# Encoder layer on one core: the first up step in two parts, and another order of VectorE's work at both phase boundaries

## The reference

```python
h = rmsnorm(x, norm1_g); proj = h @ w_in          # q, k, v, u
a = block_swept_gqa(rope(q), rope(k), v)          # 8 query heads, 2 kv heads
p = multiscale_pool(u, w_pool, pool_scale)
x = x + jnp.concatenate([a, p], axis=-1) @ w_out  # phase "out"
h2 = rmsnorm(x, norm2_g)
x = x + jnp.square(jax.nn.relu(h2 @ w_up)) @ w_down   # phases "up" and "down", hidden width 4096
```

## Time and profile before

| | us |
|---|---|
| median of 3 runs | 1525.66 |
| the profiled execution | 1525.22 |
| its span | 1523.4 |
| PE busy | 1495.4 (98%) |
| DVE busy | 1024.2 (67%) |
| ACT busy | 718.8 (47%) |
| POOL busy | 384.4 (25%) |

### The profile page before, as it was taken

How to read it: one execution, slowest core, us unless ns; L and a number is a source line. 1 busy time by engine, 2 the same in 40 slices (tenths; PEclk the granted TensorE clock), 3 DMA queues, 4 the chain that set the end, 5 groups by cost and what they waited for, 6 DMA issues and landing times.

```text
span 1523.4 us, 23325 instructions
## 1 busy us (share of the span) xinstructions
PE 1495.4 (98%) x8011; PEld 1329.0 (87%) x8011; DVE 1024.2 (67%) x1285; ACT 718.8 (47%) x1212; POOL 384.4 (25%) x340
## 2 busy tenths in 40 slices
PE   9999989999999998999999999999999999999998
PEld 8999977888878887999999999999778888888887
DVE  7434489999975667445444544548788878878875
ACT  6323289998843434455455544546233223223220
POOL 3356358888950000000000000000311311311300
PEclk9999999999999999999999999999999999999999
DMA  6110021000055747532432433338743443443434
GB/s 238 42 38 18 18 85 34 14 11 10 15 174 179 255 145 296 213 136 110 153 133 103 149 124 126 132 140 311 258 141 100 147 155 96 149 154 97 148 99 177
DMA packets 68953, 195.19 MB, mean 128 GB/s; under 512 B 5528, under 2 KB 7712, under 8 KB 68768
## 3 DMA queue, kind: packets, MB, share of 16 engines
q1 hardware_dynamic: 66832, 183.36, 34.9%
q10 hardware_dynamic: 2064, 11.08, 1.8%
HBM read 119.97 MB, written 67.63 MB: 123 GB/s over the span
## 4 chain that ended last, share of the span: by engine, by line
PE 87%; DVE 4%; POOL 3%; issue 3%; ACT 2%; DMA 0%; ACTq 0%; POOLq 0%; DVEq 0%; SPq 0%
PE ps L754 22%; PE ps L755 22%; PE ps L756 22%; PE ps L1048 5%; PE ps L929 3%; PE ps L1058 3%; PE ps L911 2%; PE ps L913 2%; PE ps L944 2%; PE ps L945 2%; POOL prob L2186 1%; DVE yacc L2024 1%; PE ps L1068 1%; DVE pTlo L1595 1%; DVE nmax L1654 1%
## 5 line engine op out<-in xcount | busy, mean ns | idle before, releaser
L754 PE MATMUL ps<-h,wuhi 128*128 128x384 f32 x896 | 300.3, 335 | 4.8 <-issue 3.8
L756 PE MATMUL ps<-h,wulo 128*128 128x384 f32 x896 | 299.9, 335 | 0.0
L755 PE MATMUL ps<-h,wuhi 128*128 128x384 f32 x896 | 299.8, 335 | 0.0
L754 PE MATMUL ps<-wdhi,hidhi 128*128 128x512 f32 x672 | 262.3, 390 | 3.7 <-DVE yacc L2024 3.7
L755 PE MATMUL ps<-wdlo,hidhi 128*128 128x512 f32 x672 | 261.5, 389 | 0.0
L756 PE MATMUL ps<-wdhi,hidlo 128*128 128x512 f32 x672 | 261.5, 389 | 0.0
L2024 DVE TENSOR_TENSOR yacc<-yacc,ps 128x1024 f32<-128x1024 f32 x168 | 204.3, 1217 | 78.1 <-PE ps L756 77.6
L1155 ACT ACTIVATE hidhi<-hin 128x1024 fp32r<-128x1024 f32 (+1 forms) x72 | 86.8, 1205 | 308.9 <-PE ps L756 298.5
L1939 DVE TENSOR_TENSOR u<-u,ps 128x384 f32<-128x384 f32 x96 | 53.1, 553 | 185.3 <-PE ps L756 185.2
L754 PEld LDWEIGHTS ps<-h,wuhi 128*128 128x128 f32 x896 | 168.8, 188 | 5.6 <-issue 5.6
L755 PEld LDWEIGHTS ps<-h,wuhi 128*128 128x128 f32 x896 | 168.8, 188 | 0.0
(11 more groups left out here) (198 smaller groups left out, 2816.2 us busy)
## 6 DMA issues: line engine op xcount, KB each, us to landing
hd<-hout SPq DMA_DIRECT2D x64, 384.0 KB, 3.3
hin<-hd SPq DMA_DIRECT2D x48, 512.0 KB, 3.8
hd<-hout SPq DMA_DIRECT2D x32, 576.0 KB, 2.8
hin<-hd SPq DMA_DIRECT2D x24, 768.0 KB, 4.4
wuraw<-in_w_up SPq DMA_DIRECT2D x17, 1024.0 KB, 6.1
wdraw<-in_w_down SPq DMA_DIRECT2D x8, 2048.0 KB, 9.5
h<-h2d ACTq DMA_DIRECT2D x7, 1536.0 KB, 13.8
xin<-in_x SPq DMA_DIRECT2D x12, 512.0 KB, 3.5
```

Of the source, the lines that this page charges most:

```text
L754: pe.matmul(out, w_hi, m_hi, start=start, stop=False, skip_group_check=resumed)
L755: pe.matmul(out, w_hi, m_lo, start=False, stop=False, skip_group_check=resumed)
L756: return pe.matmul(out, w_lo, m_hi, start=False, stop=stop, skip_group_check=resumed)
```

## The change

- PE: products 2 and 3 of step 0 are made in two parts. The first two pairs (256 columns) of both run right after the last transposes (`up_first_pairs`); the third pair (128 columns) waits for `h2_lo` as the whole product did. The banks of the up steps are numbered anew, so that product 3's bank is not one that the last transposes are read from.
- DVE in phase out, p = 10: residual 10 comes after the four sums and before the five low halves of `lo_h2(9)`; the four `sum_wu` all come after the scaling. p = 11: only weight parts 2 and 3 are split before the scaling; part 4 after it; parts 5 and 6 after `lo_h2(11)`.
- DVE in the first unit of phase down: acc 2 comes before `lo_part(0, 2)` and `lo_part(1, 0)`.
- Last product: DVE adds its q = 0 half when PE has made the first six matmuls, then the other half; SP stores the two tiles of that quarter one by one.

ACT's and POOL's lists are unchanged.

```diff
@@ -315,6 +315,8 @@
         y_in = [sem(f"y_in{u}") for u in range(UNITS)]
         down_done = sem("down_done")
+        down_half = sem("down_half")
+        acc_half = sem("acc_half")
         acc_done = sem("acc_done")
         y_out = sem("y_out")
@@ -447,7 +449,7 @@
         OPENS = (0, 1, 3)
         GATHER = (0, 1, 0, 2, 0, 2, 0)
-        UP_BANKS = ((6, 7, 5), (2, 3, 4))
+        UP_BANKS = ((6, 7, 2), (3, 4, 5))
         QUARTERS = ((0, 0), (0, 0), (1, 0), (1, 1), (1, 1), (1, 0), (0, 1))
@@ -731,16 +733,21 @@
                 for half, h in ((0, 0), (1, 1), (1, 0), (0, 1)):
                     done = max(o for o in range(SLOTS) if QUARTERS[o] == (half, h))
-                    sp.wait_ge(acc_done, SLOTS * (UNITS * (DOWNS - 1) + u + 1) + done + 1)
+                    if (u, done) == (UNITS - 1, SLOTS - 1):
+                        sp.wait_ge(acc_half, 1)
+                    else:
+                        sp.wait_ge(acc_done, SLOTS * (UNITS * (DOWNS - 1) + u + 1) + done + 1)
                     a, b = unit_tiles(u, half)
                     cols = slice(h * 512, (h + 1) * 512)
-                    if b == a + 1:
+                    if b == a + 1 and (u, done) != (UNITS - 1, SLOTS - 1):
                         sp.dma_start(y[a * P:(a + 2) * P, cols].rearrange("(q p) n -> p q n", p=P),
                                      acc_quarter(u, half, h)).then_inc(y_out, 16)
                     else:
                         for j, t in enumerate((a, b)):
+                            if j and (u, done) == (UNITS - 1, SLOTS - 1):
+                                sp.wait_ge(acc_done, SLOTS * (UNITS * DOWNS + 1))
                             sp.dma_start(y[t * P:(t + 1) * P, cols], yacc[:, u, half, j, cols]).then_inc(y_out, 16)
-            sp.wait_ge(y_out, 16 * 4 * (UNITS + 1))
+            sp.wait_ge(y_out, 16 * (4 * (UNITS + 1) + 1))
@@ -1091,16 +1098,28 @@
                 if o == 6:
                     pe.wait_ge(u_sum, 3 * s + 2)
+                pairs = slice(2, 3) if isinstance(s, int) and s == 0 and o in (2, 3) else slice(0, 3)
+                up_pairs(g, par, o, pairs).then_inc(up_done, 1)
+
+            def up_pairs(g, par, o, pairs):
+
                 for k in range(4):
-                    mm = three(up_bank(par, o), wuhi[o][:, k], wulo[o][:, k], h2[g][o][:, 0, :, k], h2[g][o][:, 1, :, k],
-                               o in OPENS and k == 0, k == 3, o not in OPENS)
-                mm.then_inc(up_done, 1)
+                    mm = three(up_bank(par, o)[:, pairs], wuhi[o][:, k], wulo[o][:, k], h2[g][o][:, 0, pairs, k],
+                               h2[g][o][:, 1, pairs, k], o in OPENS and k == 0 and pairs.start == 0, k == 3, o not in OPENS or pairs.start > 0)
+                return mm
+
+            def up_first_pairs(o):
+
+                pe.wait_ge(wu_lo, o + 1)
+                if o == 2:
+                    pe.wait_ge(u_copied, 1)
+                up_pairs(1, 0, o, slice(0, 2))
             def up_step(s, w, g, par):
...
                     up_product(s, w, g, par, o)
-            def down_product(n, z, u, o):
+            def down_product(n, z, u, o, last):
                 m = UNITS * n + u
                 if u == 0:
@@ -1117,18 +1136,22 @@
                         mm = three(banks[:, q], hidhi[i][:, k, q, j], hidlo[i][:, k, q, j],
                                    wdhi[z][o][:, k], wdlo[z][o][:, k], o in OPENS and k == 0, k == 1, o not in OPENS)
+                    if q == 0 and (u, o) == (UNITS - 1, SLOTS - 1) and last:
+                        mm.then_inc(down_half, 1)
                 mm.then_inc(down_done, 1)
-            def down_chunk(n, z):
+            def down_chunk(n, z, last=False):
                 for u in range(UNITS):
                     for o in range(SLOTS):
-                        down_product(n, z, u, o)
+                        down_product(n, z, u, o, last)
             for p in range(TT):
...
             up_product(0, 0, 1, 0, 1)
             transpose_x2(TT - 1)
+            up_first_pairs(2)
+            up_first_pairs(3)
             for o in range(2, SLOTS):
                 up_product(0, 0, 1, 0, o)
@@ -1141,7 +1164,7 @@
                 down_chunk(h * 2 + 1, 1)
                 down_chunk(h * 2 + 2, 0)
-            down_chunk(DOWNS - 1, 1)
+            down_chunk(DOWNS - 1, 1, True)
@@ -1853,7 +1876,7 @@
                                          ).then_inc(xs2_done, 1)
-            def lo_h2(p):
+            def lo_h2(p, sums=True, halves=True):
                 q = p // 2
@@ -1864,20 +1887,26 @@
                     dve.wait_ge(h2_stored[2], 32)
                 raw = {o: h2_full(q, o) for o in (2, 3, 4, 5)}
-                dve.wait_ge(xT2_done, p + 1)
-
-                dve.wait_ge(h2_b11, q + 1)
-                dve.tensor_tensor(raw[4], h2_bank(q, 2), raw[5], ALU.subtract).then_inc(h2_sum, 1)
-                dve.wait_ge(h2_sum, 4 * q + 1)
-                dve.tensor_tensor(raw[2], h2_bank(q, 3), raw[4], ALU.subtract).then_inc(h2_sum, 1)
-                dve.wait_ge(h2_sum, 4 * q + 2)
-                dve.tensor_tensor(raw[3], raw[2], raw[5], ALU.subtract).then_inc(h2_sum, 1)
-                dve.wait_ge(h2_sum, 4 * q + 3)
-                dve.tensor_tensor(raw[5], h2_bank(q, 1), raw[2], ALU.subtract).then_inc(h2_sum, 1)
-                dve.wait_ge(h2_sum, 4 * q + 4)
-                for n, o in enumerate(LATE_HALVES):
-                    dve.wait_ge(h2_hi, SLOTS * q + 3 + n)
+
+                def half(o):
+                    dve.wait_ge(h2_hi, SLOTS * q + 1 + o)
                     minus(h2_half(q, o, 1), h2_bank(q, 3) if o == 6 else raw[o], h2_half(q, o, 0)).then_inc(h2_lo, 1)
+
+                if sums:
+                    dve.wait_ge(xT2_done, p + 1)
+
+                    dve.wait_ge(h2_b11, q + 1)
+                    dve.tensor_tensor(raw[4], h2_bank(q, 2), raw[5], ALU.subtract).then_inc(h2_sum, 1)
+                    dve.wait_ge(h2_sum, 4 * q + 1)
+                    dve.tensor_tensor(raw[2], h2_bank(q, 3), raw[4], ALU.subtract).then_inc(h2_sum, 1)
+                    dve.wait_ge(h2_sum, 4 * q + 2)
+                    dve.tensor_tensor(raw[3], raw[2], raw[5], ALU.subtract).then_inc(h2_sum, 1)
+                    dve.wait_ge(h2_sum, 4 * q + 3)
+                    dve.tensor_tensor(raw[5], h2_bank(q, 1), raw[2], ALU.subtract).then_inc(h2_sum, 1)
+                if halves:
+                    dve.wait_ge(h2_sum, 4 * q + 4)
+                    for o in LATE_HALVES:
+                        half(o)
             dve.wait_ge(pv_done, seqs[1].turn(NQ // 2, 0, 0))
@@ -1914,22 +1943,26 @@
                 if p + 1 < TT:
                     split_c(p + 1)
-                lo_h2(p - 1)
-                residual(p)
                 if p == TT - 2:
+                    lo_h2(p - 1, halves=False)
+                    residual(p)
+                    lo_h2(p - 1, sums=False)
                     lo_wu(0, 0)
                     lo_wu(0, 1)
-                    sum_wu(0, 0)
-                    sum_wu(0, 1)
+                else:
+                    lo_h2(p - 1)
+                    residual(p)
                 if p == TT - 1:
-                    for o in range(2, SLOTS - 1):
-                        lo_wu(0, o)
+                    lo_wu(0, 2)
+                    lo_wu(0, 3)
                 scale_x2(p)
                 if p == TT - 2:
-                    sum_wu(0, 2)
-                    sum_wu(0, 3)
-            lo_wu(0, SLOTS - 1)
+                    for k in range(4):
+                        sum_wu(0, k)
+            lo_wu(0, 4)
             lo_h2(TT - 1)
+            lo_wu(0, 5)
+            lo_wu(0, 6)
             def sum_u(s, par, k):
@@ -2023,6 +2056,13 @@
                 dve.tensor_tensor(q, q, down_banks(u, o), ALU.add).then_inc(acc_done, 1)
+            def accumulate_halves(n, u, o):
+                q = acc_quarter(u, *QUARTERS[o])
+                dve.wait_ge(down_half, 1)
+                dve.tensor_tensor(q[:, 0], q[:, 0], down_banks(u, o)[:, 0], ALU.add).then_inc(acc_half, 1)
+                dve.wait_ge(down_done, SLOTS * (UNITS * n + u + 1) + o + 1)
+                dve.tensor_tensor(q[:, 1], q[:, 1], down_banks(u, o)[:, 1], ALU.add).then_inc(acc_done, 1)
+
             def down_chunk(n, z, last=False, first=False):
                 for u in range(UNITS):
@@ -2043,10 +2083,12 @@
                     if first and u == 0:
                         lo_wd(0, 0, 5)
+                        accumulate(n, u, 2)
                         lo_part(0, 2)
                     if more:
                         lo_part(m + 1, 0)
-                    accumulate(n, u, 2)
+                    if not (first and u == 0):
+                        accumulate(n, u, 2)
                     if first and u == 0:
                         lo_wd(0, 0, 6)
@@ -2057,9 +2099,11 @@
                     accumulate(n, u, 5)
                     lo_wds(*slots[u][2])
-                    accumulate(n, u, 6)
                     if more:
```

(3 more changed lines are left out.)

## The result

The changed kernel takes 1530.83 us (median of 8 runs, 1528.70 to 1534.78), the kernel before 1525.59 beside it (8 runs, 1524.95 to 1527.84). The ratio is 1.0033 with a 95% interval of 1.0022 to 1.0044: slower by 5.2 us, 0.33%. The forecast was 1528.4, range 1524.8 to 1531.0.

The account below looks back on a forecast made before the run. PE, busy 98% of the span, bounds the kernel, so only its waits and slow clock can be won. +4.8 - 1.0 - 1.1 = +2.7 us on 1525.22 gives 1527.9, plus 0.4 for the median: 1528.4, range 1524.8 to 1531.0.

Parts of the forecast that it names:

- The reload: First boundary, step 1: late weight splits delay the next wuraw load by 5.9 us; boundary +4.8 us net.
- Rival (a): First boundary: the wuraw load lands in about 7 us, boundary +0.8, total 1524.4 us; chance 16%.
- Step 0: First boundary: last transposes 1.1 us earlier, product 4 starts at 595.4 against 596.88, so 1.4 us comes back.
- rival (b): First boundary: PE's clock falls again just before step 1's product 2, costing 1.5 us, total 1529.9; chance 19%.
- Second boundary: Start of phase down: acc 2 moved earlier lets product 5 start 1.0 us sooner, at 1071.75.
- End: Last product: sum and store by halves shorten the tail by 1.1 us, bounds -0.5 and -1.5.

Follow-up runs that it names:

- run 1: The changed kernel with weight splits 5 and 6 put back ahead of the last tile's sums and halves: 1526.40 us, ratio 0.9998.
- run 2: The kernel before with only weight splits 5 and 6 moved behind the twelfth tile's halves: 1532.38 us, ratio 1.0041.
- run 7: The changed kernel once more, nothing altered, for a second profile: 1531.41 us, ratio 1.0041.
- run 3: The changed kernel with acc 2 of the first down unit back in its old place: 1533.24 us.
- run 8: run 1 with ACT's copy of step 0's second u bank ahead of its first square and relu: 1525.74 us, ratio 1.0000.
- run 9: run 4 plus 24 unused transposes of 8 rows in PE's program ahead of step 0's product 2: 1526.74 us, ratio 1.0006.
- run 10: run 1 with products 2 and 3 of step 0 whole again: 1523.51 us, ratio 0.9981.
- run 4: The kernel before with only acc 2 moved earlier in phase down and the last sum and store by halves: 1523.88 us, ratio 0.9985.
- run 5: The kernel before with only the last sum and store by halves: 1524.95 us, ratio 0.9991.
- run 11: run 8 plus 47 unused transposes of 8 rows after the last tile's transposes, ahead of the first part: 1526.36 us, ratio 0.9996.
- run 12: run 10 plus 50 unused transposes of 8 rows in the stand before step 0's product 2: 1525.87 us, ratio 1.0002.

## Why the prediction came out as it did

**The reload (+4.8): right, by its own chain.** Issue 593.05 (forecast near 593.5), landing after 10.49 (11.1), copy 603.62 (604.6), product 2 of step 1 at 612.20 (613.4), 1.1 given back forecast and 0.2 seen (5.04 from there to product 4 at 617.24, where it was 5.26), which the earlier product 2 made good. So two errors of about 1 cancel; that +4.81 met +4.8 so closely is luck. The piece measured +4.81 and +5.41 in two traces; runs 1 and 2 confirm the cause. Rival (a) needed a landing in 7. By the Trainium skill (DMA: Bandwidth & Descriptors, section Queues, rings and completion order) each DMA engine takes turns between queues packet by packet. Even turns would have borne out (a); the measured 10.5 and 11.1 beside the h2 loads speak against even turns, and the measurement decides.

**Step 0: right in kind.** POOL's power took 0.55 without DVE's splits beside it, as the earlier trace rows said; product 4 started 1.67 sooner, less 0.39 of scatter 1.3, forecast 1.4.

**The clock, rival (b): it came, and in this trace cost nothing that shows.** I gave 19% to a fall that costs 1.5. The clock fell twice, 0.84 and then 0.50 in the windows from 590, and 0.57 in 605 to 607.5. The first fall lay wholly ahead of the wait for the load. The second was inside two products between the load's landing and product 2, and there ACT's copies, not PE, set the time: product 2 waited 1.14 more for u. In run 7, the same kernel, the second fall came later, and there it did cost. PE waited longer before product 2, and the product itself was slow:

```profile
613.25 0.55 PE L761 MATMUL ps<-h,wuhi 128*128 128x384 f32 x1 [2.73 <-ACT u L1178]
```

The clock is 0.67 and 0.64 in the two windows from 612.5, and the piece takes 498.00 where it took 497.40; run 3's trace has the same fall (0.50 from 612.5) and 497.94. So rival (b) is in two of the three traces of this boundary, at 0.5 to 0.6 and not at 1.5. The Trainium skill (TensorE: Matmul & The Clock Gate, section HAM oscillation — how this bites in real kernels) says that bursts shorter than the waits between them begin at the slow clock each time. The trace after doesn't bear that out: in 590 to 592.5 PE was busy for all of the 2.50 while the clock fell, before the stand of 2.34, and its bursts (3.4 us from 589.51, some 8 from 595.21) are longer than its waits (0.87, 2.34, 1.77).

**Second boundary (-1.0): right in mechanism, then outweighed.** Product 5 came 1.57 sooner in its phase; I had 1.0, because I gave weight split 6 the 1.85 that it took in the earlier trace rows, and it took 1.22. That varies: in runs 1, 7, 8, 9 and 10 it took 2.04, and in run 7 product 5 was only 0.76 sooner. In the median the moved sum is worth 1.1 (run 4 less run 5). The step that failed is the one by which nothing else in phase down changes: the stand of 1.59 at 1094.35 took the gain back. I had followed the queues of data and counted the extra matmuls as PE time only. They are instructions as well, and the views of the DMA engines show instructions as transfers of 16 KB beside the data.

**End (-1.1): -1.28 in the trace, -1.4 (0 to -2.8) in run 5.**

**The parts of products 2 and 3.** I priced them at 1.4 of idle PE time and took their benefit to be the 1.4 of product 4. Run 1 against run 10 shows what they did as a whole: step 1's product 4 starts at 613.50 and 613.46, so nothing was won; in phase down they cost 2.6 (464.46 against 461.86), of which 0.7 before product 2 of the first unit and 1.75 in the stand. By medians it is 1526.40 and 1523.51, 2.5 apart when each is taken against its own "before".

**The sum.** Forecast +2.7 on the profiled execution. It showed +3.5, of which -0.39 is scatter; without that, +3.9 = 2.7 + 1.6 (the stand) less 0.4 in small terms. The medians differ by 5.2 and, in run 7's group, 5.0; run 7's own trace has, without its first piece, +4.3. Some 1 us between traces and medians stays open; the later fall of the clock (0.6 in run 7) may be part of it. Open, too, is how a single fetch of 16 KB delays a load by 2: its packet time is that of one of 16 engines for 1 us (1.5% of 16 engines in 4 us), so even a load that waited for it in full would be 1 later. That TensorE's longer program makes the stand is shown by runs 9 and 10. That it does so by the place of its fetch is argued from the two tables: in the first all early fetches belong to longer programs, and the second, for another load, has long programs with the fetch elsewhere and no delay. No run moved a fetch out of the loads behind the stand itself.

## What to carry over

Before moving an operation back in a queue, list what counts on it: here a DMA issue on another engine hung on a weight split that PE didn't need yet, and its 10.5 us beside other loads were worth more than the whole stall. Instructions added in a straight-line stretch aren't priced by their own time alone; compare the transfers of kind "instruction" of both traces in every later stretch in which DMA is full and a load is awaited. A ledger with cuts at equal instructions finds such a distant loss at once. And where a move helps in one unit, look for the same order in the next: acc 2 of the second unit still stands behind a split that waits for a load, which is where the stand came; moving it there too was not tried. Of this change, the moved sum and the end by halves should be kept (run 4, -0.15%), alone or with run 10's order (-0.19%).

## What the runs showed of the hardware

**Narrow matmuls.** Matmuls of 256 columns in the parts follow each other every 0.12, those of 128 every 0.11, and those of 384 every 0.17: per matmul two parts cost 0.23 where the whole costs 0.17.

**Idle PE time could be filled at no cost, and in one of two runs the clock stayed up.** In run 11, 47 transposes of 8 rows took 3.0 (0.064 each; the forecast's 0.081 was too high) in a place with a stand of 1.39, and nothing behind came later: from product 0 (580.68) to the wait's end at 605.91 are 25.23, in run 8 without them (581.50, 606.86) 25.36. Run 8's windows:

```profile
592.50:595.00 2.50, 2.50 (x18) 0.77 1.01 419
595.00:597.50 2.50, 2.50 (x10) 0.55 1.01 409
```

and run 11's:

```profile
592.50:595.00 2.50, 2.50 (x24) 1.00 1.02 417
595.00:597.50 2.50, 2.50 (x16) 1.00 1.06 432
```

PE ran without a pause and the granted clock stayed at 1.00. In each of the 13 other traces one of the windows of 2.5 us between 587.5 and 602.5 has 0.50 to 0.62. Run 12 is one of them: its 50 transposes left a stand of 1.09, and the clock fell all the same (0.57 in 592.5 to 595). And in run 11 it fell later, behind the stand of 2.37 in phase down (0.55 in 1089 to 1091.5).
